# Expert outputs of six passes written home as rows and gathered once, and three weight slabs under way, in the experts of a hybrid decoder step

## The reference

```python
def _moe(h, router, wg, wu, wd):
    logits = jnp.einsum('btd,de->bte', h, router).astype(jnp.float32)
    top_v, top_i = lax.top_k(logits, TOP_K)          # 2 of 8
    probs = jax.nn.softmax(top_v, axis=-1)
    combine = jnp.sum(jax.nn.one_hot(top_i, N_EXPERTS) * probs[..., None], axis=-2)
    y = jnp.zeros(...)
    for e in range(N_EXPERTS):
        y = y + combine[..., e:e + 1] * ((silu(h @ wg[e]) * (h @ wu[e])) @ wd[e])
    return y
```

## Time and profile before

| | us |
|---|---|
| median of 3 runs | 1519.98 (1518.37 to 1521.0) |
| the profiled execution | 1522.91 |
| its span, first to last instruction | 1521.1 |
| PE busy | 1486.8 (98%) |
| DVE busy | 770.0 (51%) |
| ACT busy | 342.0 (22%) |
| mean granted TensorE clock | 0.993 of full speed |

### The profile page before, as it was taken

One profiled execution on the slowest core, in us unless ns is written; L12 is line 12 of the kernel. 1 busy time (PEld: TensorE's weight loads), 2 busy tenths in 40 slices (PEclk: granted clock), 3 DMA queues, 4 the chain that ended last, 5 costly groups with the idle time before them and its releaser, 6 DMA issues.

```text
span 1521.1 us, 40728 instructions
## 1 busy us (share of the span) xinstructions
PE 1486.8 (98%) x17933; PEld 1267.2 (83%) x17933; DVE 770.0 (51%) x1700; ACT 342.0 (22%) x855; POOL 56.2 (4%) x68
## 2 busy tenths in 40 slices
PE   9999999999999999999999999999989999999987
PEld 6899976887899999998899877877977787898653
DVE  6456756746665655556367467645742221222123
ACT  2315224222112212233233323222220000010001
POOL 1000010110000000000000010200010000000000
PEclk9999999999999999999999999999999999999998
DMA  8324435213644344247425352125879999999995
GB/s 328 132 84 158 162 137 132 85 33 85 223 146 159 133 173 155 99 171 263 175 84 211 126 136 102 44 68 171 348 303 335 331 341 346 349 333 345 338 318 222
DMA packets 64334, 299.84 MB, mean 197 GB/s; under 512 B 21839, under 2 KB 23567, under 8 KB 37663
## 3 DMA queue, kind: packets, MB, share of 16 engines
q1 hardware_dynamic: 50392, 268.10, 48.5%
q0 software_dynamic: 2944, 18.09, 3.1%
q10 hardware_dynamic: 10823, 11.05, 2.8%
HBM read 277.93 MB, written 19.28 MB: 195 GB/s over the span
## 4 chain that ended last, share of the span: by engine, by line
PE 81%; DMA 14%; DVE 3%; issue 1%; ACT 1%; SPq 0%; DVEq 0%; ACTq 0%
PE ps L2111 15%; PE ps L1248 12%; PE ps L1711 9%; PE ps L1911 7%; DMA arena<-in_egu 6%; PE ps L1718 5%; DMA arena<-in_edown 5%; PE ps L1197 4%; PE ps L1823 4%; PE ps L2040 3%; DMA ring<-in_egu 3%; PE ps L1785 2%; PE ps L1210 2%; PE ps L1567 2%; DMA ring<-in_mix 1%
## 5 line engine op out<-in xcount | busy, mean ns | idle before, releaser
L1711 PE MATMUL ps<-xn,ring 128*128 128x288 f32 x576 | 155.7, 414 | 0.4 <-ACT gate L2477 0.4
L1711 PEld LDWEIGHTS ps<-xn,ring 128*128 128x128 f32 x576 | 105.7, 190 | 37.4 <-issue 10.3
L2111 PE MATMUL ps<-arena 128*128 128x144 f32 x1028 | 133.4, 285 | 1.2 <-DVE arena L3648 1.2
L2111 PEld LDWEIGHTS ps<-arena 128*128 128x128 f32 x1028 | 129.3, 189 | 1.4 <-issue 1.4
L1911 PE MATMUL ps<-y_ml,arena 128*64 128x96 f32 (+4 forms) x2688 | 111.0, 244 | 6.3 <-issue 6.3
L1911 PEld LDWEIGHTS ps<-y_ml,arena 128*64 128x64 f32 x2688 | 108.9, 137 | 9.6 <-issue 9.5
L2040 PE MATMUL ps<-arena,mixed 128*32 128x256 f32 x2024 | 113.2, 383 | 2.3 <-DMA arena<-in_edown 2.1
L2040 PEld LDWEIGHTS ps<-arena,mixed 128*32 128x32 f32 x2024 | 64.9, 111 | 46.6 <-DMA arena<-in_edown 2.6
L3572 DVE TENSOR_TENSOR mixed<-ps,mixed 128x96 f32<-128x96 f32 (+4 forms) x66 | 16.8, 254 | 131.1 <-PE ps L1911 130.8
L1911 PEld LDWEIGHTS ps<-y_ml,ring 128*64 128x64 f32 x1536 | 64.2, 139 | 9.2 <-issue 9.1
L1911 PE MATMUL ps<-y_ml,ring 128*64 128x96 f32 (+4 forms) x1536 | 67.3, 248 | 4.1 <-issue 4.1
(11 more groups left out here) (588 smaller groups left out, 2558.7 us busy)
## 6 DMA issues: line engine op xcount, KB each, us to landing
arena<-in_egu SPq DMA_DIRECT2D x56, 1024.0 KB, 6.2
ring<-in_mix SPq DMA_DIRECT2D x46, 1024.0 KB, 5.4
arena<-in_edown SPq DMA_DIRECT2D x40, 1024.0 KB, 6.2
ring<-in_mix SPq DMA_DIRECT2D x48, 768.0 KB, 4.2
ring<-in_egu SPq DMA_DIRECT2D x32, 1024.0 KB, 7.0
ring<-in_gu SPq DMA_DIRECT2D x14, 1024.0 KB, 4.7
arena<-in_gu SPq DMA_DIRECT2D x8, 1024.0 KB, 5.7
arena<-in_C POOLq DMA_DIRECT2D x2, 2048.0 KB, 7.9
```

What stands on the lines that cost most here:

```text
L1711: last = mm(ps[:, bank, 0:T], ring[:, s, P * k:P * k + P], xn[:, k, :], start=(k == 0), stop=(k == KT - 1))
L2111: last = mm(ps[:, dense_bank(side, product), 0:HALF], left, right, start=(k == 0 and product in (1, 2, 5)), stop=(k == n - 1), skip_group_ ...
```

## The change

1. `IN_FLIGHT` is 3.
2. The output of passes 0 to 5 is no longer scattered in the next pass. `down_rows` puts tokens on output partitions and the model width on columns; ACT and DVE copy it to `yg_rows`, and ACT writes it to a DRAM tensor `home_rows`, 128 rows a pass, row 0 zero.
3. DVE computes for each token and choice the row where its output lies (`row_home`; 0 if it lies in pass 6 or later).
4. In pass 6 POOL gathers these rows for the three pieces of tokens, DVE weighs and adds the two choices, PE turns the sum by transposes (home 0 behind unit 3, home 1 behind unit 5, home 2 before slab 4 of down) and DVE adds it to X.
5. Pass 6 and the later ones are scattered as before; `pick_places` runs only from pass 6 on.
6. ACT's zeroing covers row 0 and the last 32 rows of each pass of `home_rows`; DVE and POOL wait for four zeroing DMAs instead of two. Some semaphores are merged.

```diff
-IN_FLIGHT = 2
+IN_FLIGHT = 3
@@ PE
+            def home(i):
+                m, to, bank = TOK[i][1], HOME_TO[i], HOME_BANK[i]
+                pe.wait_ge(home_d.sem, i + 1)
+                if i == 1:
+                    pe.wait_ge(yg_a.sem, TURNED)
+                    pe.wait_ge(yg_d.sem, TURNED)
+                if i == 2:
+                    pe.wait_ge(home_x.sem, home_steps[1])
+                per = 512 // m if i < 2 else KT
+                for d in range(KT):
+                    last = pe.transpose(ps[:, bank + d // per, m * (d % per):m * (d % per) + m], to[0:m, P * d:P * d + P],
+                                        C("ident", m, m))
+                    if d % per == per - 1:
+                        last.then_inc(home_p.sem, 1)
@@ turned_expert
-                    if u < 2:
+                    if u < 2 and not homeward:
                         scatter(p - 1, blocks, u)
+                    if homeward and u in (3, 5):
+                        home((u - 3) // 2)
+                if homeward:
+                    pe.wait_ge(home_x.sem, home_steps[0])
+            def down_rows(p, blocks):
+                if p > 0:
+                    pe.wait_ge(yg_a.sem, p)
+                    pe.wait_ge(yg_d.sem, p)
                 for k, tiles in enumerate(DOWN):
                     slab_ = loaded(p, FT + k)
                     for t, f in enumerate(tiles):
+                        pe.wait_ge(e_hid.sem, p * FT + (f + 1))
+                        for c in range(D // 256):
+                            for b in range(blocks):
+                                w0 = D * t + 256 * c
+                                last = mm(ps[TB * b:TB * b + TB, 6 + c // 2, 256 * (c % 2):256 * (c % 2) + 256],
+                                          ehid[:, f, TB * b:TB * b + TB], slab_[:, w0:w0 + 256],
+                                          start=(f == 0 and c % 2 == 0), stop=(f == FT - 1), skip_group_check=True)
+                    last.then_inc(e_used.sem, 1)
+            def down(p, blocks, homeward=False):
+                if homeward:
+                    pe.wait_ge(home_x.sem, home_steps[1])
...
+                    if homeward and k == 4:
+                        home(2)
@@ expert, passes 0 to 5
-                            scatter(p - 1, blocks, 0)
...
-                    if f == 3 and not first:
-                        scatter(p - 1, blocks, 1)
@@ ACT
+            def downed_rows(p):
+                n = TB * token_blocks(p)
+                if p > 0:
+                    act.wait_ge(home_out.sem, 16 * p)
+                act.wait_ge(e_used.sem, p * ETURNS + ETURNS)
+                A(yg_rows[0:n, 0:D // 2], ps[0:n, 6, :], ACT.Copy).then_inc(yg_a.sem, 1)
+                act.wait_ge(yg_a.sem, p + 1)
+                act.wait_ge(yg_d.sem, p + 1)
+                act.dma_start(home_rows[1 + MB * p:1 + MB * p + n, :], yg_rows[0:n, :]).then_inc(home_out.sem, 16)
@@ ACT, zeroing
+                    act.dma_start(home_rows[0:1, :], zero[0:1, :]).then_inc(slots_zero.sem, 16)
+                    rows_, m = home_rows[1:, :].rearrange("(i p) d -> p i d", p=MB), MB - TB
+                    act.dma_start(rows_[m:MB], zero[m:MB].unsqueeze(1).broadcast_to([TB, TURNED, D])).then_inc(slots_zero.sem, 16)
@@ DVE, extra_passes (pass 0)
+                link(STT(places, chosen_rows, float(1 + MB * TURNED), chosen_rows, ALU.is_lt, MUL))
+                dve.tensor_copy(row_home[:, :], places)
@@ DVE
+            def weigh_home(i):
+                m, to = TOK[i][1], HOME_TO[i]
+                dve.wait_ge(home_in.sem, 32 * (i + 1))
+                link(TSC(to[0:m], to[0:m], q[0:m, 2, i:i + 1], None, MUL))
+                STT(to[0:m], HOME_SECOND[0:m], q[0:m, 3, i:i + 1], to[0:m], MUL, ADD).then_inc(home_d.sem, 1)
+            def add_home(i):
+                c0, m = TOK[i]
+                per = 512 // m if i < 2 else KT
+                for h in range(KT // per):
+                    dve.wait_ge(home_p.sem, ([0] + home_steps)[i] + h + 1)
+                    x = X[:, per * h:per * h + per, c0:c0 + m]
+                    TT(x, x, ps[:, HOME_BANK[i] + h, 0:per * m].rearrange("p (d t) -> p d t", d=per), ADD).then_inc(home_x.sem, 1)
@@ turned_expert (DVE)
+                    if u == 2 and homeward:
+                        weigh_home(0)
...
+                    if u == 4 and homeward:
+                        add_home(0)
+                        weigh_home(1)
+                if homeward:
+                    add_home(1)
                 hidden_rows(p, len(FPAIRS) - 1)
+                if homeward:
+                    weigh_home(2)
+                    add_home(2)
@@ POOL
+            pool.wait_ge(*extra_ok(0))
+            pool.wait_ge(slots_out.sem, 96)
+            pool.wait_ge(home_out.sem, 16 * TURNED)
+            gather_home(0, 0, HOME_TO[0])
+            gather_home(0, 1, HOME_SECOND)
+            pool.wait_ge(home_in.sem, 32)
+            gather_home(1, 0, HOME_TO[1])
+            pool.wait_ge(home_d.sem, 1)
+            gather_home(1, 1, HOME_SECOND)
+            pool.wait_ge(home_in.sem, 64)
+            pool.wait_ge(home_p.sem, home_steps[0])
+            gather_home(2, 0, HOME_TO[2])
+            pool.wait_ge(home_d.sem, 2)
+            gather_home(2, 1, HOME_SECOND)
```

More of the change, by code:

```diff
@@ L1952, in loaded, with expert @@
                 return eslab(k)
-            def expert(p, n, blocks, first):
+            def expert(p, n, first):
                 pe.wait_ge(ga_a.sem, p + 1)
@@ L2020, in turned_expert @@
                         turn_hidden(p, u - 1)
-                    if u < 2:
+                    if u < 2 and not homeward:
                         scatter(p - 1, blocks, u)
-            def down(p, blocks, turned=False):
+                    if homeward and u in (3, 5):
[6 more added lines that the diff above has]
+                    pe.wait_ge(yg_d.sem, p)
@@ new lines, in down_rows @@
+                    last.then_inc(e_used.sem, 1)
+            def down(p, blocks, homeward=False):
+                if homeward:
+                    pe.wait_ge(home_x.sem, home_steps[1])
+                for k, tiles in enumerate(DOWN):
+                    slab_ = loaded(p, FT + k)
+                    pe.wait_ge(e_rows.sem, units_turned(p, k))
+                    if k == 1:
+                        pe.wait_ge(e_hid.sem, units_done(p, len(FPAIRS) - 1))
+                        pe.wait_ge(e_rows.sem, units_turned(p, len(FPAIRS) - 3))
+                    if homeward and k == 4:
+                        home(2)
+                    for t, f in enumerate(tiles):
+                        if f == 3:
@@ L2034, in down @@
                             turn_lone(len(FPAIRS) - 1)
-                        if not turned:
-                            pe.wait_ge(e_hid.sem, p * FT + (f + 1))
                         for b in range(blocks):
@@ L2062, in experts @@
                     turn_slots(i + (FIXED + 1), LOOPW)
-                    down(i + FIXED, blocks, True)
+                    down(i + FIXED, blocks)
                 pe.wait_ge(ga_a.sem, npass + (FIXED + 1))
@@ L3564, in scattered, with expert @@
                     d = scattered_tile(4 * e + c)
-                    dve.wait_ge(sc_p.sem, p * KT + (4 * e + c + 1))
+                    dve.wait_ge(sc_p.sem, (p - TURNED) * KT + (4 * e + c + 1))
                     TT(X[:, d, :], X[:, d, :], ps[:, bank + c, 0:T], ADD).then_inc(sc_e.sem, 1)
-            def expert(p, n, blocks, first):
+            def expert(p, n, first):
                 for f in range(FT):
@@ L3572, in expert @@
                     TT(ehid[:, f, 0:n], ps[:, 2 * (f % 2) + 1, 0:n], esil[:, f % 3, 0:n], MUL).then_inc(e_hid.sem, 1)
-                    if f == 1 and not first:
-                        scattered(p - 1, 0)
                     if f == 2 and first:
@@ L3580, in expert @@
                         for v, bank in ((1, 4), (3, 6)):
-                            dve.wait_ge(rt_bc.sem, v + 1)
+                            dve.wait_ge(*rt_bc(0, v + 1))
                             dve.tensor_copy(chosen[:, v, :], ps[:, bank, 0:T]).then_inc(rt_chd.sem, 1)
-                    if f == 3 and not first:
-                        scattered(p - 1, 1)
-                    if f == 5:
-                        if first:
-                            dve.wait_ge(rt_cha.sem, 2)
-                            dve.wait_ge(rt_chd.sem, 2)
-                        pick_places(p, blocks)
             def hidden_rows(p, u):
```

115 lines of the change are left out of this document (66 added, 49 removed).

## The result

The change makes the kernel slower. Four runs of the changed kernel have a median of 1557.89 us (1556.57 to 1558.53), four of the kernel before on the same chip 1520.49 us (1518.37 to 1523.28): a ratio of 1.025 (1.0224 to 1.0273), 37 us more. Forecast were 1522 us and a range up to 1536; slower had the largest chance, 0.46, but the size is far outside.

The account below looks back on a forecast made before the run. PE's own work was taken to bound passes 0 to 6 and the transfers pass 7. The terms -22 + 24 + 2.5 + 6.5 + 2 - 11 summed to +2 us, giving 1522 us, range 1508 to 1536.

Parts of the forecast that it names:

- (a): Passes 1 to 6: six scatters of two halves each leave PE's queue, -22 us.
- (b): Down of passes 0 to 5: three-block passes use three column groups, 19.0 us instead of 14.38 each; +24, lower bound 0.
- Rival A: Down products: three column groups are as fast as four per record, no added time, 1498 us; chance 0.08.
- (c): Home turns on PE: twice 8 transposes of 128 columns and 8 of 32, +2.5 us.
- (d): Pass 6: PE stands for rows written, gathered and weighed, +6.5 us; bounds 0 and 15.
- rival C: Pass 6: the rows come home late, 3 to 4 us more for each pair, +13, 1535 us; chance 0.15.
- (e): Pass 1: PE's waits for instructions grow without the slow scatter products, +2 us; bounds 0 and some 10.
- rival E: Passes 3 to 5: busier engines delay instructions, gaps like pass 1's, +9, 1531 us; chance 0.10.
- (f): Pass 7: with three slabs under way PE no longer stands for slabs, 34.2 us instead of 45.2, -11.
- (g): Costs nothing: DVE's small operations, 0.8 MB more zeros in layer 1's mixer (5 us slack against 2 us), unpicked places.
- D: Transfers: the third slab brings no rate, 14 us more of transfers end last, 1534 us; chance 0.10.
- 0.14: Part of the forecast's own case (chance 0.40) that was counted as slower.

Follow-up runs that it names:

- before_no_scatter: The kernel before without the scatters of passes 0 to 4 (PE's products and DVE's adds left out): 1522.57 us, ratio 0.9996.
- before_three_groups: The kernel before, whose down products of passes 1, 3, 4 and 5 leave out the fourth piece of the model width: 1516.74 us, one run.
- after_two: The changed kernel with two slabs under way instead of three: 1547.31 us, ratio 1.018 against the kernel before.
- after_one_write: The changed kernel with two slabs under way, only pass 5's row write kept of six, home_rows zeroed whole: 1549.07 us, ratio 1.0156.
- after_zero_late: The changed kernel with two slabs under way, zeroing of home_rows issued by POOL at the mixer's end instead of by ACT: 1538.84 us, ratio 1.0122.
- after_home_late: The changed kernel with two slabs under way, home 0 moved behind unit 5, home 1 and 2 before down's slabs 4 and 5: 1542.68 us, ratio 1.0148.
- after_combined: The changed kernel with late zeroing on POOL, late home turns, and three slabs under way only for the last pass: 1541.8 us, ratio 1.0134.
- after_row0: The changed kernel with the zeroing of row 0 of home_rows cut in 16 pieces of 256 bytes: 1560.81 us, ratio 1.0262.
- before_late6: The kernel before with three slabs under way for the slabs of passes 6 and 7, two before: 1516.49 us, ratio 0.9959.

## Why the prediction was wrong

**(a) Scatters, -22.** As counted in PE's queue: pass 2, whose down has as many records as before, went from 62.0 to 58.4 us, a pair of 3.54. What failed is that this counts as time. before_no_scatter takes five of the six pairs away and gains 1 us of 1523, since at two slabs under way the transfers end no earlier, and the gate and up products without slow ones between them meet new gaps. The prediction had said "gained only if the transfers keep up" and then put the whole term into the sum.

**(b) Down, +24.** Right, and at the value taken: 19.19 us for 264 records in the changed kernel, shown to be the groups by the 198 records of before_three_groups. Rival A is out. The rule of the Trainium skill that the prediction names (TensorE: Matmul & The Clock Gate, Measured speedup vs the span model) agrees: a pack of three takes 219 ns here (14.45 us for 66) and a pack of four 218 (14.38 for 66); some 4 ns for a further tile do not show.

**(c) Turns home, +2.5.** 1.09 us for a turn of 128 columns at full clock, as taken, but 1.97 at the lower one, and 0.69 for that of 32 (at most 0.4).

**(d) Waits in pass 6, +6.5.** The frame was right: the rows were written 6.6 us after the end of pass 5 (6.7 forecast) and PE came to the first turn at 15.0 (14.9). The gathers failed it: they landed 14.2 us after the second issue, where the step took the 7.4 of the six scattering DMAs of pass 0 as if writes of rows bounded reads of rows. Every first pair took longer, 7.9 to 14.2 us in seven kernels and 13.3 with two slabs under way, so the third slab alone is not it; what sets the time within that range stays open. It is rival C by mechanism. Pass 6 should have been 5.5 us longer (6.5 + 2.5 - 3.5) and is 16.4 longer. Of the 10.9 us too little, 5.4 are stands (10.12 + 1.76 against 6.5), and most of the rest is the lower clock behind them, which no term had: 0.9 us in the turn, 2.1 in unit 4, and 1.5 in down (48, 80 and 48 records in 4.04, 4.52 and 2.80 us, 9.9 before). In after_two, whose first pair took about what was forecast, pass 6 is 12.9 us longer, 7.4 more than counted: its stands are 8.4 us, 1.9 above the term, and 5.0 of the 7.4 are the lower clock in turns, unit 4 and down.

**(e) and rival E, +2 and +9.** The fast passes should have come to 184.7 - 15.1 + 4 x 4.75 = 188.6 us. They took 210.2, so 21.6 us more, where 2 were in the sum and 9 in the rival. The gaps for instructions are 15.4 us longer than before (19.6 against 4.2), and the lower clock behind two of them (6.8 us from 1214.1 on, 3.4 from 1323.3 on, at half pace) costs 5.1, which neither had. The third slab makes 10.8 of the 21.6 (after against after_two; over all profiles 207.5 and 210.2 with three slabs, 197.0 to 199.8 with two) and 8.6 in the kernel before, alone. The other 10.8 are there with two slabs (8 to 11 in five kernels). They are not from the row writes (after_one_write), and they fit the lost scatters: a packet brings some 127 records, which are 4.2 us of fast products and more with scatters among them, and without these before_no_scatter lost 7.4 of its 15.1. That PE waits for instruction packets is shown, by the 123 gaps; that slow records gave the packets time is inferred from this run. Why the packets start later no row shows.

**(f) Third slab, -11.** Pass 7 took 34.3 us, forecast 34.2. But it takes 34.2 with two slabs too, once PE is late enough: 30 us in after_two. At 17 us (after_zero_late) and 23 us (after_home_late) it still took 43.1 and 41.3. As an edit of the changed kernel it costs 10.6 us. The step failed at pricing a rate for PE's last pass as if the bandwidth had no other user.

**(g) Zeros at no cost.** Wrong, by 5.5 us. The slack of DVE's wait at 741.3 was right and beside the point: the cost is in the issue on ACT, 2.69 us for one instruction at 706.1, and in PE, which stands 2.57 us for ACT and then has the lower clock, twice 3.4 us. The step looked at who waits for the transfer, not at who issues it. after_zero_late shows it: 6.5 us of start and 8.5 of time (2.9 of start in after_combined).

**The sum.** Forecast +2, measured +34.4 in the profile. The misses: start 5.5, gaps 19.6, pass 6 10.9; pass 0 was 3.4 us shorter than counted: the stand of PE while POOL issued its six DMAs did not come, though other gaps did. Together 32.6, and the rest is rounding of the passes. Pass 0 of the kernel before varies from 48 to 56 us among the runs with the same code there, by that stand and by gaps near its end, so a few us of each single profile are not the edit's. In the prediction's chances, C, D, E and 0.14 make 0.49 and not the 0.46 given for slower; it changes nothing here.

**Left open.** Why ACT's third issue takes 2.7 us; why the instruction packets start later beside three slabs; why a pair of gathers takes 7.9 us once and 14.2 another time; and whether the row way could be made level with the scatters: its best version here stayed at 1.2% above.

## What to carry to other kernels

Deepen prefetch only where the consumer really waits for it: one slab more under way won 11 us in the last pass and cost nearly as much elsewhere, and given to the last pass alone it is worth 0.5%. A term taken from a queue is worth its time only if what it ran beside (transfers, the supply of instructions) also ends earlier; and the duration of one small transfer, read once, is no bound for another: the first pair of gathers took 7.9 to 14.2 us. When a fast engine has gaps at a fixed number of records, look for its instruction packets among the DMA queues. Price a DMA on the engine that issues it too, and follow who waits for that engine.

## What the runs showed of the hardware

- A third DMA in a row on ACT's queue, behind two of 3.5 and 2.25 MB that had just been issued, took 2.63 to 2.69 us to issue in five kernels (the first two 1.13 to 1.14 together, the fourth 0.78 to 0.81, and 1.23 in after_row0), whether it moved one row or 16 shorter pieces. The issues of that stretch, KB each:

```profile
slots<-arena ACTq DMA_DIRECT2D x1, 3584.0 KB
slots<-arena ACTq DMA_DIRECT2D x1, 2304.0 KB
...
home_rows<-arena ACTq DMA_DIRECT2D x1, 768.0 KB
home_rows<-arena ACTq DMA_DIRECT2D x1, 4.0 KB
```

- PE's instructions come by DMA, in packets of 16 KB on a queue of their own, one for some 127 records. In 123 gaps of 14 kernels PE went on 1.2 to 1.6 us behind the end of such a packet, which itself took 0.97 to 1.01 us in the mean.
- With one slab of 1 MB more under way on SP's queue these gaps summed to 19.6 and 19.7 us in passes 1 to 5 of the changed kernel, against 9.9 to 12.6 in five kernels with two. In the kernel before it was 10.8 against 4.2 to 6.7 in three profiles, with one of two slabs (before_late6, three from pass 5 on) at 10.6. In pass 5 of the kernel before, 448 records without a gap became stretches of 127, one every 6.2 to 6.4 us.
- The first pair of gathers, 1 MB in all, took 7.9 to 13.3 us from the second issue beside two slabs of 1 MB under way (four kernels), and 14.2 beside three (two kernels).
- PE's last stretch of pass 1 after ran 99 records in 6.17 us instead of some 3.3. The granted clock was at the level of 1.2 GHz for 6.8 us from 1214.1 on; PE had stood 2.09, 2.16 and 3.05 us between its stretches before.
